# A hybrid mLSTM and attention layer: four half tiles of the merge as filler at the mLSTM stage's end, and two gate tiles to one more Strassen pair

## Chip, cores and metric

The kernel runs on one core of one Trainium2 chip. The metric is device time in microseconds (us); the figure of a kernel is the median of its runs. Engines are named as the profile names them: PE (TensorE, the matrix engine), DVE (VectorE), ACT (ScalarE), POOL (GpSimd), and SP (SyncE, which here only issues DMAs).

## What is computed

One layer of a diffusion backbone over 512 latent and 128 prompt tokens (640 in all, `TOK`), model width 2048, float32. A combined input projection feeds two branches: a bidirectional mLSTM (4 heads of 256) and a windowed attention (16 query heads of 64). Their outputs are projected, gated and merged:

```python
u = rmsnorm(x, norm_pre_w) * (1 + scale) + shift
aq, ak, av, az, mq, mk, mv, mo, mz, mg, ga, gb = split_proj(u, w_in)
...
y_b = att * jax.nn.silu(az)
y_a, C, n, m = mlstm_branch(mq, mk, mv, mo, mz, mg, b_gates, mlstm_norm_w, C0, n0, m0)
merged = jax.nn.sigmoid(ga) * (y_a @ w_proj_a) + jax.nn.sigmoid(gb) * (y_b @ w_proj_b)
out = rmsnorm(merged @ w_out, norm_post_w)
return x + gate * out, (k, v, C, n, m)
```

`ga` and `gb` are 2048 channels each, so the input projection has 32 gate tiles of 128 channels (16 for `ga`, 16 for `gb`).

## The kernel before

**Three-pass products.** Every float32 operand is split into a high half (a copy rounded to fp32r) and a low half (the rest): ACT writes the high halves (`XH` of activations, `WH` of weights), DVE subtracts them to get the low ones (`XL`, `WL`). A product is then XH·WH, XL·WH and XH·WL. Activations lie channel-major, 640 tokens in two PSUM banks of 320 columns, and a *half tile* is 128 output channels over 1024 input channels: 8 k steps x 3 passes x 2 banks = 48 matmuls of 320 columns. An input tile (2048 input channels) is two half tiles, x = 0 on `XH[:, 0:8]` and x = 1 on `XH[:, 8:16]`. Weights come by DMA into four slots of `RAW` (512 KB each), are split into two slots of `WH`/`WL`, and a slot of `RAW` is loaded again once its low half is done.

**Stages**, in the order of PE: 4 plain input tiles; 30 Strassen pairs (`PAIRS`), each two input tiles done as 7 products of 24 matmuls (168 instead of 192); the attention stage (`T_L1`, 14 gate tiles as filler between the attention's own instructions); the mLSTM stage (`T_L2`, 12 gate tiles, 24 half tiles, as filler between the phases of four heads); the merge; the output projection. Of the 32 gate tiles 6 lie in the last three pairs, 14 in the attention stage, 12 in the mLSTM stage. Every gate tile is evacuated by ACT (`evac`), spilled to DRAM by POOL (`spill`), and read back in the merge by POOL (`gate_b`, `gate_a`) into `Y` or a work buffer, where ACT takes its sigmoid.

**The mLSTM stage's loop.** All engines run over quarters q = 0 to 47; s = q // 2 is the half tile, and `phases(q)` gives head h phase r = q + 1 - 12h. A quarter of PE holds half of a half tile's matmuls (24) with the head's instructions around and inside them. For the last head (h = 3): q = 37 (s = 18) turns the inputs token-major and DVE and ACT prepare the decays; q = 39 (s = 19) is the score products (line 2616), DVE's weighing of the scores (line 2002, `weigh`), and inside the half tile a small product that waits for `ml_p`, the end of that weighing; q = 41 and 42 are the two read-outs, q = 43 (s = 21) the prompt's state (lines 2647 and 2635), after which DVE forms two quotients and copies the state (line 2074); q = 44 to 46 are DVE's statistics (2036), POOL's root (1017), DVE's normalisation (2081), PE's transposes (2340) and DVE's last product into `Y[:, 0:8]` (2087 and 2089). DVE's low split of the next half tile's weights (`lo`, line 1514) comes at the end of each odd quarter. Every engine works in program order, so an instruction that waits holds all behind it.

**The merge** (`w_proj_b` over `Y[:, 8:16]`, the attention's output; `w_proj_a` over `Y[:, 0:8]`, the mLSTM's). The B part is 16 half tiles (`b_product`), each followed by DVE's `b_gate(n)`, which multiplies the two banks by the sigmoid in `Y` (two instructions of 320 columns). The A part is 7 Strassen blocks (`a_product`, 7 products of 12 matmuls) and two plain half tiles. B half tiles 0 to 5 run ahead of the first block, the others between the blocks (`B_AFTER`). Before B half tile 0, `high_y` (ACT) and `low_y` (DVE) must have put the split of `Y[:, 8:16]` into `XH[:, 0:8]` and `XL[:, 0:8]`, which hold the layer's input until the last x = 0 half tile is done. PE waits for these one k step at a time (`k_wait`). The high halves are made at the mLSTM stage's end, and the first five low ones (`LOW_EARLY`) in its last quarters; DVE's program reaches them after the last head's product into `Y`. The last two half tiles of the A part take weights (`a_half`, SP line 830) that are loaded once the last block's splits are done.

Of the kernel before, what the change touches and what calls it, by code (L numbers as in the profile page):

```python
# [40 lines left out]
T_PAIR, T_L1, T_L2, T_MERGE, T_OUT, T_END = 4, 64, 78, 90, 92, 108  # L41
# [5 lines left out]
GADA_LAST = [4, 3, 3, 3, 3]  # L47
# [7 lines left out]
LOW_EARLY = 5  # L55
# [120 lines left out]
B_AFTER = [(6,), (7,), (8,), (9, 10), (11,), (12, 13), (14, 15)]  # L176
B_UNIT, A_UNIT, _u = {}, [], 0
for _n in range(2, 6):
    B_UNIT[_n], _u = _u, _u + 2
# [5 lines left out]
UNITS = _u  # L185

# [7 lines left out]
def sigmoid_b(k):  # L194


    return k + 1 if k < 3 else 2 * k - 2


def sigmoid_a(a):  # L200


    return 2 * a + 5 if a < 5 else a + 9
# [5 lines left out]
def raw_more(g):  # L209


    return 0 if g < 2 * T_MERGE + 2 else (112, 112, 224, 224)[g % 4]
# [52 lines left out]
def hybrid_layer(nc, x_prompt, x_sample, cache_k, cache_v, state_C, state_n, state_m, c, c_ctx, w_ada, b_ada,  # L265
# [12 lines left out]
    with ExitStack() as ctx:  # L278
# [220 lines left out]
        def w_slot(g):  # L499

            return g % 2 if g < 2 * T_PAIR else (g + PAIRS) % 2 if g < 2 * T_MERGE + 2 else (g + 1) % 2
# [38 lines left out]
        def unit_weights(w, u):  # L540

            return w[:, u % 4 // 2, 512 * (u % 2):512 * (u % 2) + 512]
# [5 lines left out]
        def b_bank(n):  # L548

            at = 2 * n if n < 4 else 2 * (n % 2)  # L550
            return bank[at:at + 2]
# [24 lines left out]
        def _(sp):  # L576
# [206 lines left out]
            for s in range(2 * L2_TILES * M_HEADS):  # L783
                if s > 6 and s % 6 == 4:
                    row_loads(s // 6)
                in_tile(T_L2 + s // 2, 0, COL_MERGE + P * (GATES_PAIRED + L1_TILES + s // 2), (s % 2,))
# [18 lines left out]
            def b_half(n):  # L805

                if n < 4:
                    sp.wait_ge(lo_done, 2 * T_MERGE + (n - 1 if n >= 2 else n - 3))
# [28 lines left out]
            b_half(0)  # L837
            b_half(1)
            states_out(M_HEADS - 1)
            b_half(2)  # L840
            b_half(3)
            a_pieces(0)
            b_half(4)
            b_half(5)
# [28 lines left out]
        def _(pool):  # L873
# [131 lines left out]
            for t in range(L2_TILES * M_HEADS):  # L1005
# [13 lines left out]
                spill(T_L2 + t, 0, RB_GA + GATES_PAIRED + L1_TILES + t)  # L1019


            pool.wait_ge(ml_ya, M_HEADS + 1)

            def gate_b(k):
# [4 lines left out]
                for t in range(T_L2 + row - 4, T_L2 + row - 2):  # L1029
# [13 lines left out]
            pool.wait_ge(y_lo, 8)  # L1043
            gate_b(0)
            gate_b(1)
            gate_a(0)
            gate_b(2)
            gate_b(3)
# [31 lines left out]
        def _(act):  # L1080
# [268 lines left out]

            for q in range(4 * L2_TILES * M_HEADS):  # L1350
# [15 lines left out]
            def high_y(ks, done, shift=0):  # L1366
                for k in ks:
                    nc.scalar.activation(XH[:, k, :], Y[:, (k + shift) % KT, :], ACT.Copy).then_inc(done, 1)

            act.wait_ge(yb_done, 10 * KV_HEADS + 1)  # L1370
            act.wait_ge(w_used, 2 * T_MERGE - 1)
            high_y(range(8), y_hi, 8)
# [1472 lines left out]
```

## Time and profile before

| | us |
|---|---|
| median of 3 runs | 1942.57 |
| lowest, highest | 1941.44, 1942.93 |
| the profiled execution, as timed | 1941.78 |
| its span, first to last instruction | 1940.2 |
| PE busy in it | 1909.7 (98%) |
| DVE, ACT, POOL busy | 1269.1, 693.3, 144.4 |
| mLSTM stage, start and end on PE | about 1226 and 1495 |
| merge, start and end on PE | about 1495 and 1709 |

PE is the engine to read. Its matmuls are pipelined: a row of 16 matmuls shows a little more than 16 times their pace, because the last one's end is counted with its latency; the chain of waits merges them and shows the pace itself. A time in a row's first column is the start from the span's start. "L2436" is a line of the kernel before. In the rows of the timeline a bracket tells how long the engine was idle and who released it.

### The profile page before, as it was taken

The page shows a single profiled execution, that of the slowest core. Times are in us where ns is not written, and L with a number is a line of the kernel's source. Part 1 is how long each engine was busy: PE and PEld are TensorE (multiplying, and loading weights), DVE is VectorE, ACT ScalarE, POOL GpSimd, SP SyncE. Part 2 cuts the span into 40 slices and gives each one's busy share as a digit, 9 for nine tenths or more (in the row PEclk, how much of TensorE's full clock was granted, in tenths as well). Part 3 has the DMA queues.
Part 4 walks back from the last instruction along what each step waited for, and adds up shares of the span by engine and source line. Part 5 has one row for each costly group of instructions (what it writes and reads, how often), then busy time and mean ns, then how long its engine had stood idle before and what let it go on. Part 6 is the DMA issues. An engine that isn't in the chain of part 4 may idle for free.

```text
span 1940.2 us, 31275 instructions
## 1 busy us (share of the span) xinstructions
PE 1909.7 (98%) x12182; PEld 1770.8 (91%) x12182; DVE 1269.1 (65%) x2181; ACT 693.3 (36%) x1077; POOL 144.4 (7%) x259
## 2 busy tenths in 40 slices
PE   6999999999999999999999999999999999999998
PEld 2589999999999999999998998899899999988886
DVE  3368877777777777887666665465466787663224
ACT  4453333333333333333555554232233443332221
POOL 2010010010001000100000000000000100000000
PEclk9999999999999999999999999999999999999999
DMA  9963464444444444544732422363552643524224
GB/s 368 391 205 88 135 190 135 135 146 135 135 135 146 130 132 133 159 143 130 205 95 88 132 82 88 98 160 120 125 138 73 208 144 104 177 76 141 77 76 163
DMA packets 299839, 278.43 MB, mean 144 GB/s; under 512 B 20976, under 2 KB 254184, under 8 KB 297824
## 3 DMA queue, kind: packets, MB, share of 16 engines
q1 hardware_dynamic: 279504, 199.93, 35.1%
q0 software_dynamic: 19936, 76.97, 11.2%
q8 instruction: 62, 1.02, 0.2%
q14 instruction: 33, 0.27, 0.1%
q10 hardware_dynamic: 304, 0.25, 0.0%
HBM read 237.14 MB, written 42.58 MB: 144 GB/s over the span
## 4 chain that ended last, share of the span: by engine, by line
PE 90%; DVE 4%; DMA 3%; ACT 1%; issue 1%; SPq 1%; POOL 0%; DVEq 0%; POOLq 0%; ACTq 0%
PE bank L2427 13%; PE bank L2507 12%; PE bank L2500 12%; PE bank L2501 12%; PE bank L2768 10%; PE bank L2436 7%; PE bank L2706 6%; PE bank L2710 3%; PE bank L2340 2%; PE bank L2400 2%; PE bank L2627 2%; DMA WORK<-in_w_ada_dram 2%; PE bank L2616 2%; PE bank L2568 1%; PE bank L2629 1%; PE bank L2545 1%
## 5 line engine op out<-in xcount | busy, mean ns | idle before, releaser
L1213 ACT ACTIVATE WH<-RAW 128x1024 fp32r<-128x1024 f32 x195 | 206.7, 1060 | 386.1 <-PE bank L2507 306.1
L1717 DVE TENSOR_TENSOR WL<-RAW,WH 128x1024 fp32r<-128x1024 f32 x195 | 238.4, 1223 | 68.8 <-ACT WH L1213 68.6
L2427 PE MATMUL bank<-XH,WH 128*128 128x320 f32 x1024 | 243.5, 319 | 0.9 <-issue 0.7
L1092 ACT ACTIVATE WH<-RAW 128x1024 fp32r<-128x1024 f32 x94 | 99.4, 1058 | 392.7 <-PE bank L2436 253.3
L2427 PE MATMUL bank<-XL,WH 128*128 128x320 f32 x1024 | 233.1, 309 | 0.0
L2501 PE MATMUL bank<-XL,WH 128*128 128x320 f32 x720 | 212.5, 309 | 0.0
L2500 PE MATMUL bank<-XH,WH 128*128 128x320 f32 x720 | 212.4, 309 | 0.0
L1514 DVE TENSOR_TENSOR WL<-RAW,WH 128x1024 fp32r<-128x1024 f32 x92 | 112.1, 1221 | 110.6 <-ACT WH L1092 110.4
L2427 PEld LDWEIGHTS bank<-XH,WH 128*128 128x128 f32 x1024 | 169.6, 188 | 8.7 <-issue 7.1
L2427 PEld LDWEIGHTS bank<-XL,WH 128*128 128x128 f32 x1024 | 171.3, 188 | 0.0
L2436 PE MATMUL bank<-XH,WL 128*128 128x320 f32 x1024 | 165.7, 311 | 0.3 <-DVE WL L1514 0.3
L2436 PEld LDWEIGHTS bank<-XH,WL 128*128 128x128 f32 x1024 | 153.2, 188 | 4.6 <-issue 3.8
L1761 DVE TENSOR_TENSOR OUTS<-bank,OUTS 128x320 f32<-128x320 f32 x210 | 100.4, 490 | 83.4 <-PE bank L2507 80.4
L2500 PE MATMUL bank<-TW,WH 128*128 128x320 f32 x480 | 141.8, 309 | 0.0
L2501 PE MATMUL bank<-TW,WH 128*128 128x320 f32 x480 | 141.6, 308 | 0.0
L2501 PE MATMUL bank<-TY,WH 128*128 128x320 f32 x480 | 141.6, 309 | 0.0
L2500 PE MATMUL bank<-TY,WH 128*128 128x320 f32 x480 | 141.6, 309 | 0.0
L2500 PEld LDWEIGHTS bank<-XH,WH 128*128 128x128 f32 x720 | 135.2, 188 | 0.0
L2501 PEld LDWEIGHTS bank<-XL,WH 128*128 128x128 f32 x720 | 135.2, 188 | 0.0
L2507 PE MATMUL bank<-XH,WL 128*128 128x320 f32 x720 | 120.3, 309 | 0.7 <-DVE WL L1717 0.7
L2768 PE MATMUL bank<-WH,XH 128*128 128x512 f32 x300 | 117.2, 391 | 0.6 <-DVE WL L1514 0.6
L2768 PE MATMUL bank<-WL,XH 128*128 128x512 f32 x300 | 116.7, 389 | 0.0
(279 smaller groups left out, 3626.9 us busy)
## 6 DMA issues: line engine op xcount, KB each, us to landing
RAW<-in_w_in_dram SPq DMA_DIRECT2D x165, 512.0 KB, 3.8
proj_dram<-OUTS POOLq DMA_DIRECT2D x92, 320.0 KB, 2.5
WORK<-in_w_ada_dram POOLq DMA_DIRECT2D x64, 256.0 KB, 3.6
RAW<-in_w_out_dram SPq DMA_DIRECT2D x32, 512.0 KB, 3.7
WORK<-in_w_ada_dram SPq DMA_DIRECT2D x30, 512.0 KB, 10.4
WORK<-proj_dram SPq DMA_DIRECT2D x16, 640.0 KB, 4.5
WORK<-proj_dram POOLq DMA_DIRECT2D x16, 640.0 KB, 5.4
RAW<-in_w_ada_dram SPq DMA_DIRECT2D x18, 512.0 KB, 9.3
```

The costliest lines, as they stand in the source:

```text
L1092: nc.scalar.activation(WH[:, w_slot(gs), :], RAW[:, slot, :], ACT.Copy).then_inc(hi_done, 1)
L1213: ins = nc.scalar.activation(WH[:, (j + p) % 2, :], pair_raw(j, p), ACT.Copy)
L1514: V.tensor_tensor(WL[:, w_slot(gs), :], RAW[:, gs % 4, :], WH[:, w_slot(gs), :].bitcast(F32), ALU.subtract).then_inc(lo_done, 1)
L1717: V.tensor_tensor(WL[:, w, :], pair_raw(j, p), WH[:, w, :].bitcast(F32), ALU.subtract)\
L1761: V.tensor_tensor(cols(*out), pair_bank(j, p)[:, 0:HALF_TOK], cols(*x), ALU.add).then_inc(done, n)
L2427: pe.matmul(banks[n][:, 0:HALF_TOK], wh[:, k, :], x[:, k0 + k, n * HALF_TOK:(n + 1) * HALF_TOK], start=(first and k == 0 and wi == 0), sto ...
L2436: ins = pe.matmul(banks[n][:, 0:HALF_TOK], wl[:, k, :], XH[:, k0 + k, n * HALF_TOK:(n + 1) * HALF_TOK], start=False, stop=(last and k == 7))
L2500: pe.matmul(out, wh[:, k, :], bh[:, k, :], start=(k == 0), stop=False)
L2501: pe.matmul(out, wh[:, k, :], bl[:, k, :], start=False, stop=False)
L2507: ins = pe.matmul(out, wl[:, k, :], bh[:, k, :], start=False, stop=(k == 7))
L2706: pe.matmul(out, wh[:, k, :], x[part][:, k, :], start=(first and k == 0 and part == 0), stop=False)
L2768: ins = pe.matmul(bank[(5 * n + b) % 8][:, :], x[:, kt, b * P:(b + 1) * P], w[:, k, :], start=(first and k == 0 and wi == 0), stop=(last a ...
```

## The change

Two of the twelve gate tiles of the mLSTM stage move into one more Strassen pair (`T_L1` and all later tile numbers go up by 2, `PAIRS` from 30 to 31), and the four half slots that this leaves at the mLSTM stage's end (s = 20 to 23) take B half tiles 0 to 3 of the merge. After the stage B half tiles 4 to 8 run ahead of the first Strassen block (five, where there were six), and one follows each block. The steps that these four half tiles need move with them: ACT's eight high halves to s = 19, DVE's eight low ones to q = 38, POOL's reads of the first two pairs of gates to t = 10 and 11 of its loop, their sigmoids to s = 21 and 23, and `b_gate(0)` to `b_gate(2)` to the ends of s = 21 to 23. PE waits for all eight low halves at once, and s = 22 and 23, whose banks half tiles 0 and 1 have used, wait for `b_gated`. The work on the last of the adaLN sums (`GADA_LAST`) is spread over six pairs. The core of the diff:

```diff
-T_PAIR, T_L1, T_L2, T_MERGE, T_OUT, T_END = 4, 64, 78, 90, 92, 108
+T_PAIR, T_L1, T_L2, T_MERGE, T_OUT, T_END = 4, 66, 80, 92, 94, 110
-GADA_LAST = [4, 3, 3, 3, 3]
+GADA_LAST = [3, 3, 3, 3, 2, 2]
-LOW_EARLY = 5
+L2_HALVES = 24
+L2_MERGED = 4
+L2_GATES = (L2_HALVES - L2_MERGED) // 2
+T_GATES = T_L2 + L2_GATES
+LEADS = L2_MERGED + 5
-B_AFTER = [(6,), (7,), (8,), (9, 10), (11,), (12, 13), (14, 15)]
+B_AFTER = [(9,), (10,), (11,), (12,), (13,), (14,), (15,)]
...
             for t in range(L2_TILES * M_HEADS):
                 h, k = divmod(t, L2_TILES)
+                if t == L2_GATES:
+                    pool.wait_ge(y_lo, 8)
+                if t >= L2_GATES:
+                    gate_b(t - L2_GATES)
...
             for q in range(4 * L2_TILES * M_HEADS):
                 s, part = divmod(q, 2)
                 if part == 0:
                     hi(0, 0, 2 * T_L2 + s + 1)
-                    if s % 2 == 0:
+                    if s % 2 == 0 and s <= 2 * L2_GATES:
                         evac(0, T_L2 + s // 2 - 1)
+                    if s == 2 * L2_GATES - 1:
+                        act.wait_ge(yb_done, 10 * KV_HEADS + 1)
+                        act.wait_ge(w_used, 2 * T_GATES - 1)
+                        high_y(range(8), y_hi, 8)
+                    if s > 2 * L2_GATES and s % 2:
+                        b_sigmoid(s // 2 - L2_GATES)
...
                 if part and s + 1 < 2 * L2_TILES * M_HEADS:
                     lo(0, 0, 2 * T_L2 + s + 1)
-                if q == 4 * L2_TILES * M_HEADS - 2:
-                    low_y(range(LOW_EARLY), y_hi, y_lo, 8)
+                if q == 4 * L2_GATES - 2:
+                    low_y(range(8), y_hi, y_lo, 8)
+                if part and s > 2 * L2_GATES:
+                    b_gate(s - 2 * L2_GATES - 1)
...
                 if part == 0:
-                    if x == 0:
+                    if n >= 2:
+                        pe.wait_ge(b_gated, n - 1)
+                    elif n >= 0:
+                        pe.wait_ge(out_ready, T_GATES - 1 + n)
+                        pe.wait_ge(y_lo, 8)
+                    elif x == 0:
                         pe.wait_ge(out_ready, t - 1)
                     pe.wait_ge(hi_done, 2 * t + x + 1)
-                    high_products(banks, w, 8 * x, range(0, 4), x == 0)
+                    high_products(banks, w, k0, range(0, 4), first)
```

How this stands in the instruction order of DVE, before and after, at the last head's scores (a name in brackets is the semaphore that the instruction waits for: `y_hi` counts high halves of `Y`, `ml_s` the score products). Before:

```order
L1983 COPY WORK<-bank 128x256
L1984 COPY WORK<-bank 128x256
L1514 TENSOR_TENSOR WL<-RAW,WH 128x1024 [waits hi_done]
L2002 SCALAR_TENSOR_TENSOR WORK<-bank,WORK 128x512 [waits ml_s,ml_decay]
L2002 SCALAR_TENSOR_TENSOR WORK<-bank,WORK 128x128
L2002 SCALAR_TENSOR_TENSOR WORK<-bank,WORK 128x384 [waits ml_s]
```

After:

```order
L1998 COPY WORK<-bank 128x256
L1528 TENSOR_TENSOR WL<-RAW,WH 128x1024 [waits hi_done]
L1983 TENSOR_TENSOR XL<-Y,XH 128x640 [waits y_hi] x8
L2016 SCALAR_TENSOR_TENSOR WORK<-bank,WORK 128x512 [waits ml_s,ml_decay]
L2016 SCALAR_TENSOR_TENSOR WORK<-bank,WORK 128x128
```

The eight low halves of `Y` now stand between the split for half tile 19 and the weighing of the scores.

DVE again, after the last head's prompt state (the copies of `bank` are that state). Before:

```order
L2074 COPY WORK<-bank 128x257 [waits dve_chain]
L2074 COPY WORK<-bank 128x257
L1514 TENSOR_TENSOR WL<-RAW,WH 128x1024 [waits hi_done]
L2036 BN_STATS WORK<-WORK 128x6 [waits ml_ubd]
L2036 BN_STATS WORK<-WORK 128x6 x4
```

After:

```order
L2100 COPY WORK<-bank 128x257 [waits dve_chain]
L2100 COPY WORK<-bank 128x257
L1528 TENSOR_TENSOR WL<-RAW,WH 128x1024 [waits hi_done]
L2066 TENSOR_TENSOR Y<-bank,Y 128x320 [waits sig_done,w_used]
L2066 TENSOR_TENSOR Y<-bank,Y 128x320
L2050 BN_STATS WORK<-WORK 128x6 [waits ml_ubd]
```

`b_gate(0)`, the two products into `Y`, now stands behind the split and ahead of the statistics.

PE at the same place: the end of s = 21 and the start of s = 22. Before:

```order
L2647 MATMUL bank<-WORK 128x257 [waits ml_ubd]
L2647 MATMUL bank<-WORK 128x257
L2635 MATMUL bank<-WORK 128x257 x2
L2436 MATMUL bank<-XH,WL 128x320 x8
L2427 MATMUL bank<-XH,WH 128x320 [waits hi_done,out_ready]
```

After:

```order
L2660 MATMUL bank<-WORK 128x257 [waits ml_ubd]
L2660 MATMUL bank<-WORK 128x257
L2648 MATMUL bank<-WORK 128x257 x2
L2449 MATMUL bank<-XH,WL 128x320 x8
L2440 MATMUL bank<-XH,WH 128x320 [waits hi_done,b_gated]
```

The first matmul of s = 22 waits for `b_gated`, the end of `b_gate(0)`, where it waited for an evacuation.

## Rows read from the trace of the kernel before

**Rows 1.** Page, part 1: engine, busy us, share of span, instructions.

```profile
PE 1909.7 (98%) x12182; PEld 1770.8 (91%) x12182; DVE 1269.1 (65%) x2181; ACT 693.3 (36%) x1077; POOL 144.4 (7%) x259
```

**Rows 2.** Windows: window, us, busy of PE, PEld, DVE, ACT, POOL, clock, DMA, GB/s.

```profile
1226.00:1508.00 282.00, 281.59 (x1651) 255.40 (x1650) 163.64 (x463) 81.74 (x138) 19.59 (x27) 1.00 0.45 121
1508.00:1700.00 192.00, 192.00 (x1312) 192.00 (x1311) 141.35 (x220) 79.60 (x114) 13.22 (x19) 1.00 0.50 154
```

**Rows 3.** Chain, pair stage: start us, us, what; from one product to the next.

```profile
799.87 1.17 PE bank L2507 x8
...
803.39 1.17 PE bank L2507 x8
```

**Rows 4.** Timeline, PE, end of the mLSTM stage: start us, us, engine, line, operation.

```profile
1492.17 2.51 PE L2436 MATMUL bank<-XH,WL 128*128 128x320 f32 x16
...
1501.00 2.61 PE L2436 MATMUL bank<-XH,WL 128*128 128x320 f32 x16 [0.28 <-DVE WL L1514]
```

**Rows 5.** Chain: the last head's prompt scores, and a full half tile later.

```profile
1445.48 0.44 PE bank L2616 x4
...
1503.61 4.69 PE bank L2427 x32
1508.31 2.35 PE bank L2436 x16
```

**Rows 6.** Timeline, ACT: splits of weights, high halves of Y.

```profile
1438.49 1.04 ACT L1092 ACTIVATE WH<-RAW 128x1024 fp32r<-128x1024 f32 x1
...
1487.51 5.12 ACT L1368 ACTIVATE XH<-Y 128x640 fp32r<-128x640 f32 x8
```

**Rows 7.** Timeline, DVE, last head's scores, and low halves of Y.

```profile
1443.17 0.89 DVE L2002 SCALAR_TENSOR_TENSOR WORK<-bank,WORK 128x128 f32<-128x128 f32 x2 [0.83 <-PE bank L2616]
1443.97 0.61 DVE L2006 TENSOR_SCALAR WORK<-WORK 128x256 f32<-128x256 f32 x2
...
1493.85 5.96 DVE L1969 TENSOR_TENSOR XL<-Y,XH 128x640 fp32r<-128x640 f32 x8
```

**Rows 8.** Timeline, PE, around the last head's prompt state.

```profile
1477.01 1.52 PE L2436 MATMUL bank<-XH,WL 128*128 128x320 f32 x8
```

**Rows 9.** Timeline, DVE, the same stretch, and one gating of Y.

```profile
1480.68 1.22 DVE L1514 TENSOR_TENSOR WL<-RAW,WH 128x1024 fp32r<-128x1024 f32 x1
1481.81 1.72 DVE L2036 BATCH_NORM_STATS2 WORK<-WORK 128x6 f32<-128x256 f32 x5
...
1511.68 0.89 DVE L2125 TENSOR_TENSOR Y<-bank,Y 128x320 f32<-128x320 f32 x2 [0.17 <-ACT Y L1413]
```

**Rows 10.** Timeline, DVE and the chain: first Strassen block of the merge.

```profile
1532.61 0.68 DVE L2148 TENSOR_TENSOR WL<-RAW,WH 128x512 fp32r<-128x512 f32 x1
...
1538.81 1.17 PE bank L2706 x8
```

**Rows 11.** Chain, end of the merge: start us, us, what.

```profile
1681.28 2.34 PE bank L2706 x16
```

**Rows 12.** DMA issues of the last two weight halves (line 830), with landing times.

```profile
L830 SPq DMA_DIRECT2D RAW<-in_w_proj_a_dram x2: 368/712/1055, 1679.9 to 1680.3; - x2
...
DMA to landing us min/median/max: 7.9/8.6/9.2
```

**Rows 13.** Windows after PE's last matmul: columns as in rows 2.

```profile
1932.00:1933.00 1.00, 0.77 (x4) 0.30 (x2) 0.00 (x0) 0.20 (x1) 0.00 (x0) 1.00 0.76 319
...
1935.00:1936.00 1.00, 0.00 (x0) 0.00 (x0) 1.00 (x2) 0.00 (x0) 0.00 (x0) 0.93 0.00 0
1936.00:1937.00 1.00, 0.00 (x0) 0.00 (x0) 1.00 (x1) 0.00 (x0) 0.00 (x0) 0.50 0.32 127
```

**Rows 14.** Waits of PE, the longest in mid-run: in all, times, longest, us.

```profile
PE bank L2340 <- DVE WORK L1924: 1.9, 3, 1.5
```

**Rows 15.** Timeline, PE, the start: the same matmuls at both clocks.

```profile
15.39 1.88 PE L2376 MATMUL bank<-RAW,VC 128*2 128x512 f32 x4 [0.94 <-DMA RAW<-in_w_ada_dram]
...
21.07 1.03 PE L2376 MATMUL bank<-RAW,VC 128*2 128x512 f32 x4
```

More of the change, by code:

```diff
@@ L1348, in inter, with high_y, b_sigmoid @@
                 nc.scalar.activation(ENM[:, :, :], COLH[:, :, 2:4], ACT.Exp).then_inc(ml_w, 1)
+            def high_y(ks, done, shift=0):
+                for k in ks:
+                    nc.scalar.activation(XH[:, k, :], Y[:, (k + shift) % KT, :], ACT.Copy).then_inc(done, 1)
+            def b_sigmoid(k):
+                act.wait_ge(sig_in[0], 16 * (k + 1))
+                nc.scalar.activation(y_pair(k), y_pair(k), ACT.Sigmoid).then_inc(sig_done, 1)
             for q in range(4 * L2_TILES * M_HEADS):
@@ L1363, in _ @@
                         nc.scalar.activation(MQ, MVT, ACT.Sigmoid).then_inc(ml_eg, 1)
[L1366 to L1372, printed above, removed]
-            evac(0, T_MERGE - 1)
             hi(0, 0, 2 * T_MERGE + 1)
             act.wait_ge(ml_ya, M_HEADS + 1)
-            act.wait_ge(w_used, 2 * T_MERGE)
             def unit_free(u):
@@ L2041, in statistics, with b_gate @@
                 V.tensor_scalar(MVAR[:, :, 1], MVAR[:, :, 1], EPS, None, ALU.add).then_inc(ml_var, 1)
+            def b_gate(n):
+                if n < L2_MERGED + 2:
+                    dve.wait_ge(w_used, 2 * T_GATES + n + 1)
+                else:
+                    dve.wait_ge(p_used, USED_0 + B_UNIT[n] + 2)
+                dve.wait_ge(sig_done, sigmoid_b(n // 2))
+                for h in range(2):
+                    at = Y[:, merged_row(n), h * HALF_TOK:(h + 1) * HALF_TOK]
+                    ins = V.tensor_tensor(at, b_bank(n)[h][:, 0:HALF_TOK], at, ALU.mult)
+                ins.then_inc(b_gated, 1)
             for q in range(4 * L2_TILES * M_HEADS):
@@ L2114, in b_lo @@
                                 ALU.subtract).then_inc(p_lo, 1)
-            def b_gate(n):
-                if n < 2:
-                    dve.wait_ge(w_used, 2 * T_MERGE + n + 1)
-                else:
-                    dve.wait_ge(p_used, USED_0 + B_UNIT[n] + 2)
-                dve.wait_ge(sig_done, sigmoid_b(n // 2))
-                for h in range(2):
-                    at = Y[:, merged_row(n), h * HALF_TOK:(h + 1) * HALF_TOK]
-                    ins = V.tensor_tensor(at, b_bank(n)[h][:, 0:HALF_TOK], at, ALU.mult)
-                ins.then_inc(b_gated, 1)
             def ta_sum(n):
@@ L2197, in half_gate @@
                 V.tensor_tensor(y, y, gate, ALU.add).then_inc(merged, 1)
-            low_y(range(LOW_EARLY, 8), y_hi, y_lo, 8)
             lo(0, 0, 2 * T_MERGE)
+            b_gate(L2_MERGED - 1)
             lo(0, 0, 2 * T_MERGE + 1)
@@ L2256, in _ @@
                     b_lo(n, 1)
-            b_gate(14)
             lo(0, 0, 2 * T_MERGE + 2)
@@ L2661, in _ @@
                 t, x = T_L2 + s // 2, s % 2
+                n = s - 2 * L2_GATES
                 banks, w = bank[2 * (t % 2):2 * (t % 2) + 2], w_slot(2 * t + x)
+                k0, first, last = 8 * x, x == 0, x == 1
+                if n >= 0:
+                    banks, k0, first, last = bank[2 * (n % 2):2 * (n % 2) + 2], 0, True, True
                 for h, r in phases(q):
@@ L2693, in _ @@
                 if part == 0:
-                    high_products(banks, w, 8 * x, range(4, 6), x == 0)
+                    high_products(banks, w, k0, range(4, 6), first)
                 else:
-                    low_products(banks, w, 8 * x, x == 1, range(4, 8)).then_inc(w_used, 1)
+                    low_products(banks, w, k0, last, range(4, 8)).then_inc(w_used, 1)
             def unit(u, terms):
@@ L2747, in a_product @@
                 unit(A_UNIT[a] + p, [(a_bank(p), x, True, True)])
-            for n in range(6):
+            for n in range(L2_MERGED, LEADS):
                 b_product(n)
```

147 lines of the change are left out of this document (74 added, 73 removed).

## The prediction, made before the changed kernel was timed

> **What bounds the kernel now.** I read the page's engine shares first: PE is busy 98% of the span, DVE 65%, ACT 36% [rows 1]. Windows by stage then show that the two stages the change touches are full: PE is busy 281.59 of 282 us in the mLSTM stage and its end, and all of 192 us of the merge [rows 2]. So a matmul that goes shortens the kernel by its own pace, and a wait that comes lengthens it by its own length. The pace is in the chain of waits: a product of the pair stage has 24 matmuls and the next ends 3.52 us later [rows 3], so one is 0.1467 us; a half tile is 4.69 + 2.35 = 7.04 us [rows 5]. Last I read the timelines of PE, DVE and ACT over the last head, since the change puts new work between instructions that wait for one another there.
>
> **What goes.** Two gate tiles in the mLSTM stage are 4 half tiles, 192 matmuls; as a pair they are 7 x 24 = 168. The four merge half tiles only change places. 24 matmuls less, at 0.1467 us: **-3.52 us**. Bytes, evacuations and spills stay as they are.
>
> The old wait ahead of B half tile 0 goes too. PE's last low products of the stage end at 1492.17 + 2.51 = 1494.68, and B half tile 0, which follows, ends with its low products at 1501.00 + 2.61 = 1503.61. It took 8.93 us where 7.04 suffice [rows 4, 5]. That is 1.89 us, lost because PE followed DVE's low halves of `Y` one by one. After the change these are made in q = 38, long before. **-1.89 us**. Together -5.41.
>
> **First new wait: the last head's scores.** ACT ends the split for half tile 20 at 1438.49 + about 0.97 = 1439.5; then come the eight high halves of `Y`, 0.63 us each [rows 6], the first one there at about 1440.2. DVE is free, but each low half takes it 0.735 us (5.88 for eight, as the next starts before the last one's shown end) [rows 7], longer than ACT takes, so it has all eight at 1440.25 + 5.9 = 1446.2. Only then may it weigh the scores. Before, it had weighed three of the four blocks by then while PE made them, and the last one took 1443.17 to 1443.97, 0.80 us [rows 7]; now the four are done in a row, 3.2 us, to 1449.4. PE wants `ml_p` for the prompt's scores at 1445.48 and did not wait for it before [rows 5]. The wait is 3.9 us. After a wait PE also has to fill: 16 matmuls took 2.61 us after the short one at 1501.00, 2.35 in the flow [rows 4, 5], so 0.26 more. **+4.2 us**. The bounds: 0 if DVE could be free of the low halves by 1445.48 less 3.2, and 6 if the low halves go at the shown 5.96 and wait for ACT between. I take the worked value, all its terms being rows of the same stretch. Nobody else is late by it: DVE's next steps, the scaled queries and the split for half tile 20, come later by the same amount, and PE wants them only after 32 more matmuls and then finds itself later by 4.2 us too.
>
> **Second new wait: the banks of half tile 20.** s = 22 writes the banks of s = 20, so its first matmul waits for `b_gate(0)`. In the program of DVE this is behind the last head's two quotients, the copies of the state and the split for s = 22. By the old times PE ends s = 21 at 1477.01 + 1.52 = 1478.53 [rows 8], and ran straight on. DVE begins the split at 1480.68, is at the next instruction at 1481.81, and a gating takes 0.89 us [rows 9]: 1482.7. The wait is 4.2 us, plus the fill of 0.26: **+4.5 us**. Bounds: the split's and the gating's rows alone (1.1 + 0.9, 2.0 us) if the quotients were hidden, 5.5 if the gating also waits for its sigmoid. The sigmoid should be there: POOL's read of the gates is issued once the low halves are done, and ACT has nothing else to do at s = 21. Walking DVE's new order on by the durations of its rows, I find `b_gate(1)` done some 0.9 us before PE asks for it at s = 23, since the second wait has put PE back, and `b_gate(2)` and `(3)` 1 to 2 us before; they cost nothing.
>
> **The lead into the Strassen blocks.** One half tile less, 7.04 us, covers the preparation of `Y[:, 0:8]`. Before, DVE began its first low split of block 0 at 1532.61 and PE the block at 1538.81, 6.2 us [rows 10]. Walking the new order of DVE and ACT in the same way, the split is there some 3 us before PE wants it, and that of the third product 2 us. I take nothing, and up to 2 us if a load of weights lands late.
>
> **Third new wait: the last two weight halves.** They are issued at 1679.92 (the first) and land 7.9 us later, at 1687.8, behind the loads of the adaLN sums [rows 12]. The last block ends at 1681.28 [rows 11]. Before, two B half tiles (14.08 us) lay between it and the product that needs them; now one, so PE wants the split at 1688.3, and ACT can give it at 1687.8 + 1.04 = 1688.9 [rows 6]. 0.5 us and the fill: **+0.8 us**; bounds 0 and 2.1 (if the half that took 9.2 us is the first).
>
> The extra pair costs its matmuls and nothing else: the pair stage runs without a wait on PE at its turns [rows 3], and DVE's share of adaLN work in the last pairs gets smaller.
>
> **Sum:** -3.52 - 1.89 + 4.2 + 4.5 + 0.8 = **+4.1 us**. The profiled execution was timed at 1941.78 us; the median of the runs is 0.8 above it, and the difference is put on the median: 1942.57 + 4.1 = **1946.7 us**.
>
> **The clock.** In the middle of the run PE never idled over 1.5 us at once on the waits listed [rows 14] and its clock stayed at full; after its last matmul, at 1932.77, the granted clock fell to 0.5 within the window that starts at 1935, some 3.1 us later [rows 13]. The two new waits are longer than that. If the clock falls to 1.2 GHz in one, the matmuls behind it run slow until it rises again: at the start four matmuls took 1.88 us at the low level and 1.03 at the full one [rows 15]. Slow work of 3 us (I estimate about as much as the idle time before it) costs 1.4 us, at both waits 2.8; the bound above is 8 us of it, which is how long the start was slow, 3.7 us. The Trainium skill, TensorE: Matmul & The Clock Gate, in its section on the HAM clock gate, says that the throttled state is the default and activity releases it, and warns of idle gaps in the middle of a kernel. By that rule this change does harm at just these two places; no row here shows such a fall in mid-run.
>
> **Rivals.**
> - *The clock falls* (above). For it: waits of 3.9 and 4.2 us against 3.1 at the end. Against it: they are barely longer. 1948.1 to 1950.4, slower.
> - *Only one of the two long waits comes.* Not slower. Its place is the last head's scores: if DVE gets the low halves done before PE has made the scores, 4.2 us go, and the time is 1942.5, no change. It decides at 1442.2: if the eighth low half is there by then, PE does not wait. Against it: ACT is busy with the last head's exponents until 1438.49 [rows 6], and eight low halves need 5.9 us. The other wait could shrink alike, to about 2 us (1944.2).
> - *The change gives what its matmuls promise.* Both long waits hidden: 1942.57 - 5.4 + 0.8 = 1938.0, faster. It would need PE's 1.2 us of low products at s = 21 to cover 5.4 us of DVE's work, against the rows.
> - *The lead is too short or the last loads late.* 2 to 4 us more, 1948.7 to 1950.7.
>
> **How the numbers follow.** A measurement of this kernel can tell about 0.2%, 3.9 us, from no change: slower is above 1946.5, faster below 1938.7. The sum holds with 0.45 (its own range 1945.2 to 1948.2; somewhat over half of it above 1946.5), the fallen clock 0.22, one wait hidden or halved 0.18, the short lead 0.08, the full gain 0.07. Slower is 0.25 + 0.22 + 0.08 = 0.55, the same 0.20 + 0.18 = 0.38, faster 0.07. The range leaves out the full gain and the tails: 1942.3 to 1950.4.
>
> **What the new profile would show.** Among PE's waits a row for the weighing of the scores (the product of 128 columns behind it) near 4 us, one for a gating of `Y` near 4, one for ACT's split at the merge's end below 1, and none for low halves of `Y`. 31 pairs of 24.64 us. The granted clock below 1 in the last head would be the first rival. I am wrong if the first two waits are absent or below 2 us, or if a new one stands between the last B lead and the first block.

## The result and the profile after

| | before | changed |
|---|---|---|
| time, us, median (from, to) | 1942.77 (1941.44 to 1943.18), 6 runs | 1952.81 (1951.40 to 1954.10), 6 runs |
| the profiled execution, and its span | 1941.78, 1940.2 | 1953.34, 1951.2 |
| mean granted clock of TensorE | 0.999 | 0.996 to 0.997 in all six |

The changed kernel takes 1.0052 times as long, 95% interval 1.0042 to 1.0062: 10.0 us more. Forecast were 4.1 us more, 1946.7 us in a range of 1942.3 to 1950.4; the side is right, the size is not.

The page of the changed kernel, part 1 (engine, busy us, share, instructions), against [rows 1]: 24 matmuls fewer, TensorE busy for as long as before, the span 11 us longer.

```profile
PE 1909.9 (98%) x12158; PEld 1771.5 (91%) x12158; DVE 1279.7 (66%) x2191; ACT 693.9 (36%) x1073; POOL 144.2 (7%) x259
```

The waits of TensorE in the changed kernel (engine, what, released by: us in all, times, longest):

```profile
PE bank L2629 <- DVE WORK L2016: 4.6, 1, 4.6
PE bank L2440 <- DVE Y L2066: 4.2, 1, 4.2
...
PE bank L2353 <- DVE WORK L1938: 1.8, 2, 1.6
...
PE bank L2558 <- DVE TY L1894: 1.1, 1, 1.1
...
PE bank L2440 <- ACT WH L1106: 0.7, 1, 0.7
```

The first two and the last are the three new waits of the forecast: scores for `ml_p`, the banks for `b_gate(0)`, the late weight halves. The wait for `TY`, in the attention stage, was not forecast.

The same stretch in windows (columns as in [rows 2]: window, us, busy of the engines, granted clock, DMA share, GB/s). The clock column is the news:

```profile
1473.00:1475.00 2.00, 0.00 (x0) 0.00 (x0) 2.00 (x6) 0.00 (x0) 0.00 (x0) 0.77 0.20 42
1475.00:1481.00 6.00, 4.80 (x19) 4.80 (x20) 5.60 (x12) 1.35 (x3) 0.00 (x0) 0.51 0.01 1
1481.00:1515.00 34.00, 30.64 (x171) 28.17 (x169) 14.29 (x55) 7.22 (x8) 3.41 (x5) 1.00 0.38 120
1515.00:1522.00 7.00, 6.15 (x23) 6.15 (x24) 5.61 (x19) 0.11 (x1) 1.19 (x1) 0.51 0.13 29
1522.00:1530.00 8.00, 8.00 (x58) 7.88 (x57) 4.73 (x7) 2.22 (x2) 0.00 (x0) 1.00 0.11 33
```

The level is 1.2 GHz (0.50 in this column) for some 6.8 us at each wait: it falls while TensorE still idles (at about 1474.1 and 1515.0), and by the low shares of these windows it is back at about 1480.9 and 1521.9, so it is down for 4.7 and 6.0 us of TensorE's work, which resumes at 1476.20 and 1515.85. What that does to the matmuls stands in the chain (start us, us, what):

```profile
1466.98 5.97 DVE XL L1983 x8
1472.95 3.20 DVE WORK L2016 x8
...
1476.20 1.22 PE bank L2629 x4
1477.42 2.13 PE bank L2449 x8
1479.55 4.18 PE bank L2440 x24
...
1513.86 1.13 DVE WL L1528
1515.00 0.81 DVE Y L2066 x2
...
1515.85 6.48 PE bank L2440 x24
```

The four score matmuls took 0.44 us before [rows 5]; the eight low products take 1.18 and the 24 high ones 3.52 at the full level [rows 3]. Behind the first wait these are 7.53 us instead of 5.14, 2.4 us lost; behind the second 6.48 instead of 3.52, 3.0 us lost. The chain also shows where the first wait comes from: eight low halves in one piece, then the four blocks' weights in a row. Idle time and slow work together are 7.0 us at the first wait and 7.2 at the second.

### The profile page after: what moved, and what is told of

Read it like the earlier page. It is cut to its first block, busy times and chain, and to the rows that moved or that the text cites. A ratio compares the mean times of both kernels' runs of the same rounds, so it can differ in the third digit from the quotient of the medians.

```text
span 1951.2 us, 31270 instructions
## 1 busy us (share of the span) xinstructions
PE 1909.9 (98%) x12158; PEld 1771.5 (91%) x12158; DVE 1279.7 (66%) x2191; ACT 693.9 (36%) x1073; POOL 144.2 (7%) x259
## 4 chain that ended last, share of the span: by engine, by line
PE 89%; DVE 4%; DMA 3%; ACT 1%; issue 1%; SPq 1%; POOL 0%; DVEq 0%; POOLq 0%; ACTq 0%
PE bank L2440 13%; PE bank L2520 13%; PE bank L2513 13%; PE bank L2514 13%; PE bank L2791 10%; PE bank L2449 7%; PE bank L2728 5%; PE bank L2732 2%; PE bank L2353 2%; PE bank L2413 2%; PE bank L2640 2%; DMA WORK<-in_w_ada_dram 2%; PE bank L2581 1%; PE bank L2642 1%; PE bank L2558 1%; PE bank L2389 1%
## 5 line engine op out<-in xcount | busy, mean ns | idle before, releaser
L1227 ACT ACTIVATE WH<-RAW 128x1024 fp32r<-128x1024 f32 x202 | 214.1, 1060 | 400.7 <-PE bank L2520 318.2
L1731 DVE TENSOR_TENSOR WL<-RAW,WH 128x1024 fp32r<-128x1024 f32 x202 | 246.8, 1222 | 71.5 <-ACT WH L1227 71.2
L2440 PE MATMUL bank<-XH,WH 128*128 128x320 f32 x1024 | 245.0, 321 | 5.6 <-DVE Y L2066 4.2
L1106 ACT ACTIVATE WH<-RAW 128x1024 fp32r<-128x1024 f32 x94 | 99.3, 1058 | 403.4 <-PE bank L2449 266.0
L2440 PE MATMUL bank<-XL,WH 128*128 128x320 f32 x1024 | 234.8, 311 | 0.0
L2514 PE MATMUL bank<-XL,WH 128*128 128x320 f32 x744 | 219.5, 309 | 0.0
L2513 PE MATMUL bank<-XH,WH 128*128 128x320 f32 x744 | 219.5, 309 | 0.0
L1528 DVE TENSOR_TENSOR WL<-RAW,WH 128x1024 fp32r<-128x1024 f32 x92 | 112.1, 1220 | 109.8 <-ACT WH L1106 109.6
L2440 PEld LDWEIGHTS bank<-XH,WH 128*128 128x128 f32 x1024 | 171.9, 190 | 12.8 <-issue 7.6
L2440 PEld LDWEIGHTS bank<-XL,WH 128*128 128x128 f32 x1024 | 173.0, 190 | 0.0
L2449 PE MATMUL bank<-XH,WL 128*128 128x320 f32 x1024 | 166.7, 312 | 0.0
L2513 PE MATMUL bank<-TW,WH 128*128 128x320 f32 x496 | 146.5, 309 | 0.0
L2514 PE MATMUL bank<-TW,WH 128*128 128x320 f32 x496 | 146.4, 308 | 0.0
L2514 PE MATMUL bank<-TY,WH 128*128 128x320 f32 x496 | 146.3, 309 | 0.0
L2513 PE MATMUL bank<-TY,WH 128*128 128x320 f32 x496 | 146.3, 309 | 0.0
L2513 PEld LDWEIGHTS bank<-XH,WH 128*128 128x128 f32 x744 | 139.6, 188 | 0.0
L2514 PEld LDWEIGHTS bank<-XL,WH 128*128 128x128 f32 x744 | 139.6, 188 | 0.0
L2520 PE MATMUL bank<-XH,WL 128*128 128x320 f32 x744 | 124.3, 309 | 0.6 <-DVE WL L1731 0.6
```

Of the source, the lines that this page charges most:

```text
L1106: nc.scalar.activation(WH[:, w_slot(gs), :], RAW[:, slot, :], ACT.Copy).then_inc(hi_done, 1)
L1227: ins = nc.scalar.activation(WH[:, (j + p) % 2, :], pair_raw(j, p), ACT.Copy)
L1528: V.tensor_tensor(WL[:, w_slot(gs), :], RAW[:, gs % 4, :], WH[:, w_slot(gs), :].bitcast(F32), ALU.subtract).then_inc(lo_done, 1)
L1731: V.tensor_tensor(WL[:, w, :], pair_raw(j, p), WH[:, w, :].bitcast(F32), ALU.subtract)\
L2440: pe.matmul(banks[n][:, 0:HALF_TOK], wh[:, k, :], x[:, k0 + k, n * HALF_TOK:(n + 1) * HALF_TOK], start=(first and k == 0 and wi == 0), sto ...
L2449: ins = pe.matmul(banks[n][:, 0:HALF_TOK], wl[:, k, :], XH[:, k0 + k, n * HALF_TOK:(n + 1) * HALF_TOK], start=False, stop=(last and k == 7))
```

## The experiments

All runs stand beside runs of the kernel before on the same chip (its medians there: 1942.61, 1942.58 and 1942.85 us). My theory: the loss is two waits and, at each, the low clock behind it. The rivals: idle time alone counts; the loss lies elsewhere (attention start, last weight halves); or a wait that goes is replaced by the next.

**gate_early: the first two gates ahead of what they waited behind, on DVE.**

```diff
                 s, part = divmod(q, 2)
+                if part and s in (2 * L2_GATES + 1, 2 * L2_GATES + 2):
+                    b_gate(s - 2 * L2_GATES - 1)
                 for h, r in phases(q):
...
-                if part and s > 2 * L2_GATES:
+                if part and s > 2 * L2_GATES + 2:
                     b_gate(s - 2 * L2_GATES - 1)
```

> The changed kernel with one thing moved: on DVE the first two gates of the merged half tiles (`b_gate(0)`, `b_gate(1)`, two 128x320 multiplies each) stand ahead of the last head's prompt quotients and ahead of its scaling, where DVE is idle 6.32 and 1.32 us in the changed kernel, and no longer behind the quotients, the state copies and the weight half. Theory 1 (a wait costs its idle time and the low clock after it): TensorE's wait of 4.2 us at half tile 22 and the stretch at the low clock behind it both go, in all 7.2 us by the chain of waits (10.68 us from the first wait's row to the same place, against 3.52 before): 1952.8 - 7.2 = 1945.6 us; the granted clock rises by half of what separates the two kernels. Theory 2 (only idle time counts, the rest of the loss lies elsewhere): -4.2 us, 1948.6 us. Theory 3 (the gate's place is taken by what is late next: the second gate, or the state copies that half tile 23's products wait for): a new wait of 1 to 3 us at half tile 23, 1947 to 1950 us.

Measured: 1946.16 us (11 runs), 1.0018 times before (1.0009 to 1.0027): 6.65 us less than the changed kernel. The second wait is gone from TensorE's list, and the granted clock stays full there; of the new waits it has

```profile
PE bank L2631 <- DVE WORK L2016: 4.3, 1, 4.3
...
PE bank L2442 <- ACT WH L1106: 1.2, 1, 1.2
```

```profile
1505.00:1530.00 25.00, 24.88 (x166) 24.17 (x165) 19.06 (x46) 8.31 (x9) 1.95 (x2) 1.00 0.38 101
```

4.2 us of idle time can't give 6.65: idle time alone is out as the whole cause, unless something else got better. Theory 1 is within 0.6 us; the last wait is 0.5 us longer here, and the products behind the first wait take 8.17 us where the changed kernel's take 7.53, though that wait is 0.3 us shorter. The second gate is in time, so theory 3 doesn't hold for this edit.

**low_split: the eight low halves of `Y` in pieces, and TensorE waits for them one by one.**

```diff
                 for i in range(NB):
+                    if h == M_HEADS - 1 and i >= 2:
+                        low_y((i - 2,), y_hi, y_lo, 8)
...
                         scaled_queries(1)
+                        if last:
+                            low_y((2, 3), y_hi, y_lo, 8)
                         prompt_p(h)
+                        if last:
+                            low_y((4, 5), y_hi, y_lo, 8)
                         scaled_queries(0).then_inc(ml_qs, 1)
+                        if last:
+                            low_y((6, 7), y_hi, y_lo, 8)
...
-                if q == 4 * L2_GATES - 2:
-                    low_y(range(8), y_hi, y_lo, 8)
...
-                        pe.wait_ge(y_lo, 8)
...
                 for k in ks:
+                    if k_wait is not None:
+                        pe.wait_ge(k_wait, k + 1)
```

> The changed kernel with the eight low halves of the first eight latent rows (`low_y`, 5.97 us on DVE in one piece ahead of the last head's score weights) taken apart: two between the weights of the four blocks, two behind the first scaled queries, two behind the prompt's weights, two at the end; TensorE's half tile 20 waits for them one by one instead of for all eight. The second wait stays. Theory 1: the score weights end when the scores allow, TensorE's wait of 4.6 us for the prompt's scores goes with the low clock behind it (12.15 us from DVE's 1471.58 to the read-out against 5.14 before, 7.0 us in all): 1952.8 - 7.0 = 1945.8 us. Theory 2 (idle alone): -4.6 us, 1948.2 us. Theory 3 (the wait moves on: half tile 20 now waits for single rows, or the read-out for the scaled queries): what is left is worked out from DVE's load, 13.8 us of work in the 13.2 us from 1464.0 to where the read-out would begin: 0.6 to 2 us of new waits, 1946.5 to 1948 us.

Measured: 1944.74 us (11 runs), 1.0013 times before (1.0004 to 1.0022): 8.1 us less than the changed kernel. From 1440 to 1530 us TensorE has one wait left, and the wait for the scores has not moved on to single rows or scaled queries:

```profile
PE bank L2449 <- DVE Y L2068: 4.2, 1, 4.2
```

It gave 1.1 us more than theory 1 has. A part is in the chain behind the wait that stayed: the 24 products take 5.33 us there, not 6.48, though the wait is as long as in the changed kernel.

```profile
1507.99 5.33 PE bank L2449 x24
```

**both_moved: the two edits together.**

> Both moves together: gates early and low halves taken apart; nothing else differs from the changed kernel. Theory 1: both losses go, 1952.8 - 14.2 = 1938.6 us, that is 4.2 us under the kernel before (1942.8): the 3.52 us of matmuls saved and the 1.89 us of the old wait come out at last, less about 1.5 us that came in at the start of the attention stage. The granted clock's mean is back at 0.999. Theory 2 (idle alone): 1952.8 - 8.8 = 1944.0 us. Theory 3 (what is late next): 1941 to 1943 us, with waits of 1 to 2 us in the rows of the read-out or of half tile 23.

Measured: 1939.82 us (11 runs), 0.9985 times before (0.9976 to 0.9994): 13.0 us less than the changed kernel, 2.8 us less than before. TensorE has no wait between 1440 and 1530 us. In the chain the products behind the last head's prompt scores are back at their pace, and DVE's timeline shows why it has time: a low half fills each pause that it otherwise spends waiting for the next block of scores.

```profile
1471.01 0.44 PE bank L2640 x4
1471.45 1.18 PE bank L2460 x8
1472.63 3.52 PE bank L2451 x24
```

```profile
1465.26 0.89 DVE L2018 SCALAR_TENSOR_TENSOR WORK<-bank,WORK 128x384 f32<-128x384 f32 x2 [0.75 <-PE bank L2640]
1466.08 0.82 DVE L1983 TENSOR_TENSOR XL<-Y,XH 128x640 fp32r<-128x640 f32 x1
1466.97 0.89 DVE L2018 SCALAR_TENSOR_TENSOR WORK<-bank,WORK 128x256 f32<-128x256 f32 x2
1467.78 0.82 DVE L1983 TENSOR_TENSOR XL<-Y,XH 128x640 fp32r<-128x640 f32 x1
```

Theory 2 (1944.0) is out by 4.2 us, theory 1 (1938.6) by 1.2. So these two places hold the loss. Alone the edits gave 6.65 and 8.1 us, 14.7 together; 1.15 of the 8.1 comes from the slow stretch behind the second wait, which low_split did not touch and gate_early takes away whole, so the two sums overlap there.

**fill_first: the first wait kept, and TensorE kept at useless work in it.** This separates the clock from the idle time, since the wait can't end sooner.

```diff
+FILLERS = 28
...
                 if r == 4:
+                    if h == M_HEADS - 1:
+                        wl = WL[:, w_slot(2 * T_GATES - 1), :].rearrange("p (k n) -> p k n", k=8)
+                        pe.wait_ge(out_ready, T_GATES - 1)
+                        for m in range(FILLERS):
+                            pe.matmul(bank[m % 2][:, 0:HALF_TOK], wl[:, m % 4, :], XH[:, 8 + m % 4, 0:HALF_TOK],
+                                      start=True, stop=True)
                     pe.wait_ge(ml_p, h + 1)
```

> The changed kernel with 28 useless matmuls (128x320, about 0.147 us each at the full clock, 4.1 us) put on TensorE into its first wait, ahead of the semaphore of the last head's score weights; they write two banks that are free there, and nothing reads what they write. The wait itself can't end earlier: the score weights come from DVE at the same time. Theory 1 (the loss is idle time plus the low clock that follows it): the granted clock stays at its full level in this stretch, the products behind the wait run at 0.293 us a pair instead of 0.533, and the kernel is 2.4 us faster though TensorE does 4.1 us more work: 1952.8 - 2.4 = 1950.4 us; the second wait is as before. Theory 2 (the low clock has another cause than idle TensorE, such as what DVE or the loads do there): the level falls all the same, 1952.8 us or a little more. Theory 3 (the fillers overrun the wait because they run late or slow): slower by 0.5 to 2 us than 1952.8.

Measured: 1950.48 us (5 runs), 1.0041 times before (1.0027 to 1.0055): 2.3 us less than the changed kernel with 28 matmuls more in it. Windows and chain:

```profile
1466.00:1481.00 15.00, 14.63 (x91) 13.45 (x90) 12.71 (x24) 5.16 (x9) 1.26 (x2) 1.00 0.31 74
1510.00:1518.00 8.00, 6.17 (x24) 6.17 (x25) 6.61 (x20) 1.09 (x1) 1.19 (x1) 0.57 0.11 33
```

```profile
1474.31 0.71 PE bank L2630 x4
1475.02 1.17 PE bank L2450 x8
1476.19 3.52 PE bank L2441 x24
```

The level stays at 1.00 where the idle time is filled, and falls at the second wait, where it isn't. Of the wait for `ml_p` 0.4 us is left idle, so theory 3 (fillers that overrun) falls; DVE's work and the loads are of the same kind and amount, so theory 2 falls. In the chain the products behind the wait take 5.40 us instead of 7.53, 2.1 less. The total, 2.3 us less, agrees but is weaker evidence: these are five runs, 1949.02 to 1953.09 us, and their interval overlaps that of the changed kernel (1.0042 to 1.0062).

**gate_mid and gate_near: the second wait made shorter.** In the first, `b_gate(0)` stands behind the prompt quotients, ahead of the state copies; in the second ahead of the second quotient. `b_gate(1)` stays behind the weight half in both.

The edit of gate_mid, then that of gate_near; both also take `b_gate(0)` from its old place (last lines of the first):

```diff
                         chain.link(quotient(ab[1], NB, 1))
+                        if h == M_HEADS - 1:
+                            b_gate(0)
                         for cc in range(2):
...
-                if part and s > 2 * L2_GATES:
+                if part and s > 2 * L2_GATES + 1:
                     b_gate(s - 2 * L2_GATES - 1)
```

```diff
                         chain.link(quotient(ab[0], NB, 0))
+                        if h == M_HEADS - 1:
+                            b_gate(0)
                         chain.link(quotient(ab[1], NB, 1))
```

> The changed kernel with the first gate alone moved by a little: behind the last head's prompt quotients, ahead of the two state copies (0.76 us) and the weight half (1.22 us) that stand before it now. TensorE's wait at half tile 22 becomes 4.2 - 1.9 = 2.3 us. Theory 1a (the clock falls only in a wait as long as 4.2 to 4.6 us): the wait costs its 2.3 us, the clock stays at 2.4 GHz behind it, and the 3.0 us lost at the low clock go as well: -4.9 us, 1947.9 us. Theory 1b (the clock falls in a wait of 2.3 us just as well): -1.9 us, 1950.9 us, with the same low stretch of the granted clock in the records. Theory 2 (idle time alone counts): -1.9 us too, but then the clock's records show no low stretch, or one that costs nothing.

Measured: 1949.16 us (5 runs), 1.0036 times before (1.0022 to 1.0050), 3.65 us less than the changed kernel: between 1a (4.9) and 1b (1.9), in five runs whose interval overlaps that of the changed kernel, so the trace has to decide. The waits, and the windows around them:

```profile
PE bank L2631 <- DVE WORK L2016: 4.3, 1, 4.3
PE bank L2442 <- DVE Y L2066: 2.4, 1, 2.4
```

```profile
1475.00:1479.00 4.00, 3.34 (x14) 3.34 (x15) 4.00 (x11) 0.00 (x0) 0.00 (x0) 0.57 0.01 2
1512.00:1517.00 5.00, 4.25 (x18) 4.26 (x19) 4.75 (x16) 1.82 (x2) 0.09 (x1) 0.66 0.20 56
```

A wait of 2.4 us brought the clock down too: 0.66 over 5 us is 3.4 us at the half level, and the 24 products behind it took 5.32 us, 1.8 over. The wait of 4.3 us, too, had only 3.4 us of low clock here: the products behind it took 6.77 us instead of 7.53. Of the gain, 1.8 us is idle time, 1.2 the shorter slow stretch behind the second wait, and 0.8 lies at the first wait, which the edit did not touch.

> The changed kernel with the first gate moved ahead of the second of the last head's prompt quotients: it ends at about 1512.7 us instead of 1515.8, and TensorE's wait at half tile 22 becomes 1.1 us. Theory 1a (a wait so short leaves the clock at its full level, as the waits of 1.6 us in the attention stage do in the traces of both kernels): -3.1 us of idle time and -3.0 us at the low clock: 1952.8 - 6.1 = 1946.7 us, within 0.6 us of the run with the gates early. Theory 1b (what brings the clock down there is how little TensorE did in the whole stretch before, not the wait alone, so that 1.1 us more is enough): a low stretch of 3.4 us as in the run with the wait of 2.4 us, 1948.4 us.

Measured: 1950.86 us (5 runs), 1.0040 times before (1.0026 to 1.0053): 4.2 us more than theory 1a. The clock's part of 1a held at the gates; what failed is what I took as unchanged. TensorE waits twice:

```profile
1512.56 0.56 PE L2442 MATMUL bank<-XH,WH 128*128 128x320 f32 x2 [1.11 <-DVE Y L2066]
1522.95 0.56 PE L2442 MATMUL bank<-XH,WH 128*128 128x320 f32 x2 [2.22 <-DVE Y L2066]
```

```profile
1505.00:1530.00 25.00, 21.67 (x143) 20.81 (x142) 17.63 (x45) 5.60 (x5) 2.08 (x3) 1.00 0.26 97
```

The first wait is 1.1 us as worked out. But TensorE then comes to half tile 23 early enough to wait 2.2 us for `b_gate(1)`, which had been hidden behind the longer first wait. In gate_early it was moved as well, and no such wait came. Neither of these two waits lowered the clock. So 2.2 us did not and 2.4 us did, in one trace each; from where on it falls is not settled by these runs. Of the 4.2 us, 2.2 are this new wait, 0.6 the products behind the first wait (8.11 us, against 7.53), 0.6 the last wait (1.3 us, against 0.7); the rest is within the spread of five runs.

**gsum_late: the last weight halves.** Both edits, and one line on POOL, which holds back the four loads and the two that POOL issues behind them:

```diff
+            pool.wait_ge(hi_done, 2 * T_MERGE + 3)
             for m in range(4):
                 pool.dma_start(GS[:, :, 512 * m:512 * m + 512],
```

> Both moves, and POOL's four loads of the gate sums (2 MB in all) wait until the first of the last two weight halves of the merge has been read, instead of starting 3 us ahead of those halves' loads. Theory 1 (the last weight halves land late, 7.8 us after their issue, because the gate sums' loads run beside them): they land 1 to 2 us earlier, TensorE's wait of 0.6 us for the high half goes, and the kernel is 0.6 to 0.9 us faster than with both moves alone: 1939.0 us. Theory 2 (the halves' loads are late for their own issue or for the output weights' loads behind them): the wait stays, 1939.8 us. Theory 3 (the gate sums then come late, or slow the output weights): DVE's bias sum, at 1715.5 us with loads done long before, is hit only if the loads take over 20 us; not expected.

Measured: 1938.91 us (11 runs), 0.9980 times before (0.9971 to 0.9989); 0.9 us less than both_moved, and the fastest of all. ACT's timeline shows the first split at 1688.32 us, with the loads issued at 1683.34:

```profile
1688.32 1.06 ACT L1107 ACTIVATE WH<-RAW 128x1024 fp32r<-128x1024 f32 x1 [6.46 <-PE bank L2744]
```

In both_moved the same split waits for its load until 1690.81, with the issue at 1682.99:

```profile
1690.81 1.06 ACT L1106 ACTIVATE WH<-RAW 128x1024 fp32r<-128x1024 f32 x1 [9.30 <-DMA RAW<-in_w_proj_a_dram]
```

Some 5 us from issue to split instead of 7.8, and TensorE's wait for it is gone. Theory 1 holds as to the wait; of the total, 0.9 us, the intervals of the two runs overlap.

**before_gsum_late: the same line in the kernel before, and one more trace of it.**

> The kernel before with POOL's loads of the gate sums held back as in the run of that name on the changed kernel; nothing else. It serves two questions. First, what the late weight halves cost in the kernel before: its trace shows no wait of TensorE for a high half there, so theory 1 is that nothing is gained, 1942.6 us within 0.5; theory 2, that the fills behind those halves are shorter too, 0.5 to 1 us less. Second, the start of the attention stage, which this edit doesn't touch: one more trace of the order of before. If its length from the stage's first product to the transposes that wait for the rotated keys is a property of the kernel, it is 28.6 us again; if it spreads with the loads as in the variants of the changed kernel (28.64 to 30.16 us), the 1.5 us more in the changed kernel's profiled execution is mostly that one execution's.

Measured: 1942.36 us (11 runs), 0.9999 times before (0.9990 to 1.0008): nothing gained, as theory 1 has it. There the second B half tile covered the loads.

**tail_before: the conditioning's rows spread as before over the last pairs** (both edits in as well).

```diff
-GADA_LAST = [3, 3, 3, 3, 2, 2]
+GADA_LAST = [2, 2, 3, 3, 3, 3]
```

> Both moves (the gates early, the low halves taken apart), and the list that spreads the gate work of the conditioning over the last pairs made [2, 2, 3, 3, 3, 3] in place of [3, 3, 3, 3, 2, 2]: the last four pairs carry three rows each, as in the kernel before. It asks where the attention stage's start lost time: from the stage's first product to the transposes that wait for the rotated keys it took 28.57 us before, and 30.16, 30.07, 30.06, 29.23 and 29.40 us in the five traces of the changed kernel and its variants. Theory 1 (the shorter tail of the list moves stores and loads against one another in the last two pairs, and the keys' and queries' loads land late for it): 28.6 us again, DVE's wait for them 2.7 us instead of 3.4 to 4.3, and 0.8 us off the total: 1939.0 us. Theory 2 (it is the loads' own spread from run to run, or comes with the extra pair): the stretch stays at 29.2 to 30.2 us and the total at 1939.8 us within 0.5.

Measured: 1939.37 us (11 runs), 0.9984 times before (0.9975 to 0.9993), 0.45 us under both_moved, less than can be told apart. The stretch was 975.41 - 945.96 = 29.45 us, not 28.6: theory 1 falls. With before_gsum_late (950.64 - 921.83 = 28.81) and the others there are two traces of the old order, 28.57 and 28.81 us, and nine of the new, 28.64 to 30.16 us, 29.49 in the mean. The 1.6 us of the changed kernel's profiled execution is the largest of the nine. What goes with it is DVE's wait for the rotated keys' load, changed kernel against fill_first:

```profile
959.94 0.69 DVE L1883 TENSOR_TENSOR Y<-Y,WORK 128x512 f32<-128x512 f32 x1 [4.29 <-DMA WORK<-proj_dram]
```

```profile
958.07 0.69 DVE L1884 TENSOR_TENSOR Y<-Y,WORK 128x512 f32<-128x512 f32 x1 [2.75 <-DMA WORK<-proj_dram]
```

In fill_first, whose program is the changed one up to there, the stretch is 28.64 us. Most of it is thus the spread of these loads; whether the 0.8 us between the means belongs to the change stays open, and its cause with it.

## Why the prediction was right and wrong

**What bounds it, and what goes: right.** -3.52 and -1.89 us were there, by these rows. A merge half tile behind the mLSTM stage is 4.69 + 2.35 us again with no wait for low halves. From one and the same product ahead of the pairs (at 48.56 and 48.61) to the attention stage's first it took 921.39 - 48.56 = 872.83 us before and 945.97 - 48.61 = 897.36 after: 24.5 us for the extra pair, 24.64 in the prediction. TensorE's busy time shows the gain where no slow stretch hides it: 1909.7 us before, 1905.7 in both_moved, the first run in which it comes out. Not all of it does: between the two profiled spans lie 3.1 us, where -5.4 with 0.8 for the attention stage's start and 0.6 for the third wait gives 4.0; the other 0.9 us is not accounted for.

**First new wait: right in place and cause, 0.7 us too small.** Forecast 3.9 us, measured 4.6 in the profiled execution and 4.3, 4.3 and 4.5 in gate_early, gate_mid and gate_near. The last head's rows, loaded from DRAM, reached DVE later against TensorE than before, and all behind them with it. Before, and in the changed kernel:

```profile
1430.54 0.90 DVE L1990 TENSOR_TENSOR WORK<-WORK,CK 128x128 f32<-128x128 f32 x4 [5.31 <-DMA WORK<-rrow_dram]
```

```profile
1457.34 0.90 DVE L2004 TENSOR_TENSOR WORK<-WORK,CK 128x128 f32<-128x128 f32 x4 [6.01 <-DMA WORK<-rrow_dram]
```

DVE's wait for them is 0.7 us longer. From there to ACT's split for half tile 20, which stands ahead of the high halves, it is 7.95 us in both (1438.49 and 1465.29). The steps of DVE were as stated, 5.97 and 3.20 us. The fill of 0.26 us that the prediction adds to each wait is misread: 2.61 is a timeline row, which holds the last matmul's latency, and 2.35 the chain's pace; the row to compare is 2.51 [rows 4], so the fill is 0.10. In gate_near the 24 products behind the wait of 1.1 us take 3.62 us against 3.52, which is 0.10 again.

**Second new wait: right.** Forecast 4.2 us, measured 4.2, with DVE's order as walked. That `b_gate(1)` costs nothing was right too, and for the reason given, that the second wait has put TensorE back: gate_near took that reason away and it cost 2.2 us.

**Third new wait: right in mechanism.** Forecast 0.5 us, measured 0.7 in the profiled execution and between 0.6 and 2.3 us in the other traces that keep it. The prediction named the loads beside it, and gsum_late shows that holding them back removes it.

**The lead into the Strassen blocks: right**, no wait there.

**The clock: this step failed, twice.** The low clock was priced as a rival at 1.4 us a fall, with a chance of 0.22, and put at nothing in the sum, when it is a part of it: the level fell at both waits of the profiled execution, and all six runs show the lower mean clock. It cost 2.4 and 3.0 us. fill_first shows it alone: DVE holds TensorE back as long, 0.4 us of it is idle, the level stays full, and the products behind take 2.1 us less. The chance failed on how [rows 13] were read. After the last matmul the level was down some 3.1 us into the idle time; waits of 3.9 and 4.2 us are longer, and "barely longer" is no evidence against a fall. The waits of up to 1.5 us that left it up [rows 14] bear on a short wait only. The price failed because slow work was taken as long as the idle time before it, 3 us; it was 4.7 and 6.0 us, 10.7 in all, where the bound beside it took 8. The low level at the start [rows 15], on which price and bound rest, was read from the matmuls' times; the granted clock of that trace reads 1.00 from 8 to 31 us. The times bear the reading out: in the low stretches of the changed kernel, where the granted clock shows 0.50, two products of 320 columns start 0.53 us apart instead of 0.29, nearly the same ratio. Half of the slow work is lost: 2.35 and 3.0 us, which is what the chain has. The Trainium skill, TensorE: Matmul & The Clock Gate, in its section on HAM oscillation, reckons the extra time as the throttled time times the half that the clock lacks. By that rule the 6.8 us at each wait would cost 3.4 us; the traces show 2.4 and 3.0, since the level falls while TensorE still idles, and that part of the low time costs nothing. The warning that the prediction cited, of idle gaps in the middle of a kernel, the windows bear out: the level fell at these two waits, at the five others of 4.2 to 4.5 us in the traces of the experiments, and at one of 2.4 us.

**The sum again.** From the forecast 4.1 us: the clock adds 2.4 + 3.0, less the 0.52 of fill in the two terms, 4.9; the first wait 0.7; the start of the attention stage 0.8 by the means of the traces. That is 10.5 us against 10.0 measured. That it comes so near is in part luck: the price of the same fall spread from 1.6 to 3.0 us between traces. The range ended at 1950.4 because it is the sum with 3.7 us on it, the bound of 8 us of slow work counted once for both waits; counted at each it would have ended at 1954.1 and held the 1952.8.

## What to carry to other kernels

Where TensorE is busy all the time, price a new wait as its idle time plus the slow work behind it; waits of 4.2 to 4.6 us cost 5.9 to 7.5 here, where the clock fell. Before moving work into a stage as filler, look at the other engines' order: what was handed to DVE in one piece (eight low halves) or behind unrelated steps (the gate) made both waits, and taking it apart and moving it forward turned 10.0 us of loss into 2.8 us of gain (3.7 with POOL's loads held back) without one operation fewer than in the changed kernel. When one wait is shortened, walk on to the next user of the same engine, which it may have been hiding.

## What the runs showed of the chip

- The granted clock was low for about 6.8 us or for 3.4 us, and not by the length of the wait: waits of 4.2 to 4.6 us show both (0.51 over 7 us in the changed kernel, 0.57 over 4 us in gate_mid). The 24 products behind took 6.48 and 5.33 us after two waits of 4.2 us. The 36 behind the first wait took 7.53, 8.17, 6.77 and 8.11 us in the changed kernel, gate_early, gate_mid and gate_near (waits of 4.6, 4.3, 4.3 and 4.5 us), and 5.14 before.
- A wait of 2.4 us lowered it once, waits of 2.2 and 1.1 us did not.
- 28 useless matmuls in a wait kept the granted clock at 1.00, and the products behind it took 5.40 us instead of 7.53.
- The same load of the same program, up to there, kept DVE waiting 2.75 to 4.29 us in different executions.
